# Two gaps between on-chip buffers: a split activation tensor begins 64 bytes later

## What is computed

```python
z = u @ w_in                                       # 2048 x 11264
merged = gate_a * (y_a @ w_branch_a) + gate_b * (y_b @ w_branch_b)
h = h + merged @ w_out                             # 2048 x 2048
h = h + jnp.square(jax.nn.relu(u @ w_up)) @ w_down # 2048 x 8192 x 2048
proj = jnp.einsum('bld,dc->blc', hn, w_in[layer])  # 2048 x 6656
y = jnp.einsum('blc,cd->bld', jnp.concatenate([ya, yb], axis=-1), w_out[layer])
```

## Time and profile before

| | |
|---|---|
| Median of 3 runs | 1893.94 us |
| Lowest, highest | 1893.53, 1894.71 us |
| Profiled execution, first to last instruction | 1893.3 us |
| TensorE matmuls busy | 1879.6 us (99%) |
| VectorE, ScalarE, GpSimd busy | 1101.4, 889.3, 143.6 us |
| Mean granted TensorE clock | 0.999 |
| DMA | 346.47 MB, 183 GB/s |

### The profile page before, as it was taken

The page is one execution under the profiler, slowest core; times in us unless marked ns, Lnnn a source line. Parts: engine busy times, 40 slices in busy tenths (PEclk is TensorE's granted clock), DMA queues, the critical chain, the costliest instruction groups (busy, mean ns, idle before and its releaser), DMA issues.

```text
span 1893.3 us, 33876 instructions
## 1 busy us (share of the span) xinstructions
PE 1879.6 (99%) x13432; PEld 1743.7 (92%) x13432; DVE 1101.4 (58%) x1270; ACT 889.3 (47%) x1171; POOL 143.6 (8%) x122
## 2 busy tenths in 40 slices
PE   9999999999999999999999999999999999999998
PEld 9989998999999889988998899899889999899986
DVE  6556766667655555545445445445565556767664
ACT  6544444455544445443444344334454355664543
POOL 2001322411001100000010000000010000000000
PEclk9999999999999999999999999999999999999999
DMA  8566565566565656656665665566556655354454
GB/s 270 184 181 177 181 179 178 165 200 180 168 231 191 214 186 179 194 198 192 196 192 193 194 191 194 194 190 190 189 185 181 179 170 150 105 147 144 156 190 143
DMA packets 176434, 346.47 MB, mean 183 GB/s; under 512 B 10976, under 2 KB 11184, under 8 KB 175776
## 3 DMA queue, kind: packets, MB, share of 16 engines
q1 hardware_dynamic: 174176, 337.76, 57.2%
q0 software_dynamic: 2128, 6.82, 1.4%
HBM read 342.44 MB, written 2.10 MB: 182 GB/s over the span
## 4 chain that ended last, share of the span: by engine, by line
PE 97%; DVE 1%; ACT 0%; DMA 0%; issue 0%; SPq 0%; DVEq 0%; ACTq 0%
PE ps L446 58%; PE ps L458 33%; PE ps L548 1%; PE ps L781 1%; DVE wlo L1301 1%; PE ps L771 1%; PE ps L748 1%; PE ps L791 0%; DMA raw<-in_w_in_dram 0%; ACT whi L899 0%; PE ps L476 0%; PE ps L759 0%; PE ps L599 0%; PE ps L591 0%; DVE xlo L1323 0%; PE ps L610 0%
## 5 line engine op out<-in xcount | busy, mean ns | idle before, releaser
L1301 DVE TENSOR_TENSOR wlo<-raw,whi 128x1024 fp32r<-128x1024 f32 x631 | 796.5, 1268 | 698.1 <-ACT whi L899 697.1
L899 ACT ACTIVATE whi<-raw 128x1024 fp32r<-128x1024 f32 x631 | 664.5, 1058 | 886.3 <-PE ps L446 551.5
L446 PE MATMUL ps<-xhi,whi 128*128 128x256 f32 (+1 forms) x1904 | 542.2, 285 | 0.4 <-DVE wlo L1301 0.3
L446 PE MATMUL ps<-xhi,wlo 128*128 128x256 f32 (+1 forms) x1904 | 531.3, 279 | 0.0
L446 PE MATMUL ps<-xlo,whi 128*128 128x256 f32 x1664 | 462.5, 278 | 0.0
L446 PEld LDWEIGHTS ps<-xhi,whi 128*128 128x128 f32 x1904 | 359.1, 189 | 9.3 <-issue 6.7
L446 PEld LDWEIGHTS ps<-xhi,wlo 128*128 128x128 f32 x1904 | 357.8, 188 | 0.0
L446 PEld LDWEIGHTS ps<-xlo,whi 128*128 128x128 f32 x1664 | 313.4, 188 | 1.5 <-issue 0.7
L446 PE MATMUL ps<-x2hi,whi 128*128 128x256 f32 x1024 | 282.8, 276 | 0.0
L446 PE MATMUL ps<-x2hi,wlo 128*128 128x256 f32 x1024 | 282.7, 276 | 0.0
L446 PE MATMUL ps<-x2lo,whi 128*128 128x256 f32 x1024 | 282.7, 276 | 0.0
(11 more groups left out here) (373 smaller groups left out, 2370.6 us busy)
## 6 DMA issues: line engine op xcount, KB each, us to landing
raw<-in_w_in_dram SPq DMA_DIRECT2D x279, 512.0 KB, 3.8
raw<-in_w_up_dram SPq DMA_DIRECT2D x128, 512.0 KB, 3.7
raw<-in_w_down_dram SPq DMA_DIRECT2D x128, 512.0 KB, 3.7
raw<-in_w_out_dram SPq DMA_DIRECT2D x64, 512.0 KB, 3.8
raw<-in_w_branch_a_dram SPq DMA_DIRECT2D x16, 512.0 KB, 4.9
raw<-in_w_branch_b_dram SPq DMA_DIRECT2D x16, 512.0 KB, 3.8
x_nat<-in_x_dram SPq DMA_DIRECT2D x4, 512.0 KB, 7.4
rel<-in_rel_turned_dram POOLq DMA_DIRECT2D x8, 256.0 KB, 4.3
```

What stands on the lines that cost most here:

```text
L446: ins = mm(outs[b], w[:, k % SLOTS, j, cols], v, start=start, stop=last and j == CK - 1 and i == 2, skip_group_check=True)
L899: f(whi[:, k % SLOTS], raw[:, k % SLOTS], ACT.Copy).then_inc(whi_ready, 1)
L1301: tt(wlo[:, k % SLOTS], raw[:, k % SLOTS], whi[:, k % SLOTS], ALU.subtract).then_inc(wlo_ready, 1)
```

## The change

`x_place` grows from 48 to 64 elements per partition (192 to 256 bytes) and `arena_place` (64 bytes) goes. `xhi` and `xlo` so begin 64 bytes later. Everything behind them stays where it was, and no instruction, wait or load changes but for the addresses of x.

```diff
@@ -35,8 +35,7 @@
 CK = 2
 NC = KT // CK
 SLOTS = 4
-X_PLACE = 48
-ARENA_PLACE = 16
+X_PLACE = 64
 LEAD = 4
 TW = 320
 WIDE_FIRST = 12
@@ -127,7 +126,6 @@
         sb("x_place", [P, X_PLACE])
         xhi = sb("xhi", [P, KT, TM], F32R)
         xlo = sb("xlo", [P, KT, TM], F32R)
-        sb("arena_place", [P, ARENA_PLACE])
         x_flat = [v[:].rearrange("p k t -> p (k t)") for v in (xhi, xlo)]
         uhi, ulo = [v[:, 0:KT * T].rearrange("p (k t) -> p k t", k=KT) for v in x_flat]
         mhi, mlo = [v[:, KT * T:KT * TM].rearrange("p (k m) -> p k m", k=KT) for v in x_flat]
```

## The result

The change makes the kernel slower: 1923.53 us (1922.66 to 1923.82, five runs) against 1893.53 (1892.09 to 1894.71, five runs), a ratio of 1.0155, 95% interval 1.0143 to 1.0167. That is 30.0 us, where I had forecast 7.1. The profiled execution took 1923.53 us and spans 1921.3, 28.0 more than the span before.

What follows compares the result with a forecast made beforehand. The prediction took TensorE's matmul spacing to bound the kernel. From a median of 1893.9 us it added 7.1 us for long fast spells of x, all else 0, giving 1901.0 us; range 1887 to 1911.

Steps and rivals of the forecast that it cites:

- What bounds the kernel: TensorE's matmuls, busy 1879.6 of 1893.3 us; only their spacing or holes between them could move the time by much.
- Places: Modulo 256 bytes, rings begin at 0, x and the arena at 192; the change takes x to the rings' 0.
- Instructions, writers, cost 0: No instruction, wait or queue changes; ScalarE's and VectorE's writes of x cost 0, within 0.6 us either way.
- Streams of x: TensorE's 256-column matmuls reading x: 1,608 in long fast spells go from 113.4 to 117.8 ns, 7.1 us more.
- slow stretches: Runs of x matmuls already at 117.8 ns, 1,488 in all, were to stay slow; 6.5 us off if they sped up.
- short chunks: Pieces of x matmuls between attention steps, said to be set anew each time and left out of the sum.
- wide stage: 144 matmuls of 272 columns at 123.3 ns, 10.0 above their columns' 113.3; used only to size x's possible loss, 11.6 us.
- natural chunks: 768 matmuls of 512 columns streaming a ring over x were to stay; bound 3.4 us more.
- The bounds: For streamed x: 6.5 us off if the slow spacing went, 15.4 us more if all 3,504 fast matmuls became slow.
- x2 "stays": Sign of being right: x2's streamed matmuls in the feed-forward keep 87.07 us for 768.
- The reason I gave: Slower likelier: streams beginning at one place have the least distance, and 3,504 fast matmuls can rise, 1,488 slow ones fall.
- Its rival: Place doesn't matter to TensorE's matmuls: 1893.9 us, between 1892.5 and 1895.5; chance 0.30.

Runs made afterwards that it cites:

- the second version: The first version with three spare transposes added at the start of feed-forward quarters 2 to 4; 1897.80 us, ratio 1.0020 to the kernel before.
- the first version: The kernel before with the feed-forward's hidden layer and `yt`, which only natural chunks read, moved to offset 0 modulo 256; 1900.41 us, ratio 1.0030.

## Why the prediction was wrong in size

**What bounds the kernel** was read rightly: with TensorE busy nearly throughout, 28.3 us more of its busy time became 28.0 us of span.

**Places.** The sizes were right, with the arena at 192. The experiment that moved the rings shows what they decide: the relation of the streamed buffer to the ring sets the pace.

**Instructions, writers, cost 0:** right. `xhi`'s first blocks are written as before (median 482 ns), by this line on the tile `xhi` in the kernel after:

```profile
L925 ACT ACTIVATE xhi<-ps,mix_w x16: 458/482/539, 7.4 to 19.5; 128x256 fp32r<-128x256 f32 x16
```

**Streams of x, the step that failed.** I wrote: "I take the value between: the long fast spells of x [...] go to the slow one." I let the change choose only between the two spacings that the trace held, 113.4 and 117.8. It brought a third, 120.0, and for all x matmuls. So the term of 1,608 x 4.4 = 7.1 us was too small in its price and in its count. The same matmuls paid 6.6 ns, 10.6 us. The slow stretches, which I left slow, paid 2.2 more, 2.5 us. The short chunks, which I left out as "set anew each time", paid as well: 2.1 us before the branches, and 5.5 in the second block, whose score matmuls with 64 rows stayed at 0.66 us a group. The branches' 168 added 1.1. With the terms below (the wide stage's 2.8, natural chunks' -1.6, x2's 5.1) and the 0.2 us earlier start, this adds up to 27.9 of the 28.0 us of span.

**The bounds.** My bound for the streams took the matmuls at 113.4 ns to 117.8 (15.4) and stopped there; 6.6 ns for 3,504 and 2.2 for 1,488 would have been 26.4. I had a row for a larger excess, the wide stage's 10.0 ns, and used it for a smaller number than the known spacing gave, when it could have told me that spacings beyond the two exist.

**The wide stage** had no term. It grew by 3.1 ns a matmul, 2.6 us in the piece of 840 and 2.8 in all.

**Natural chunks:** I bounded them by 0 and 3.4 us more. They gained 2.1 ns each, 768 x 2.1 = 1.6 us less.

**x2 "stays":** true of three quarters, wrong of the first, where a slow spell was caught on entry for 5.1 us. I had the rows for it in the spells of the earlier trace rows, but I asked only of the stages that read x which spell they would be in.

**The reason I gave** for more time rather than less was two streams with the least distance at one place. It is half right at best: 0 is the slowest of the six for streamed x, but 64, 128, 160 and 224 are slow too, and at one place the natural form is at its quickest. What the six places show is that 192 was the odd one out, not that 0 was. The direction was right with this reason, and so partly by luck.

**The rule weighed against it** was the second, independent read port for the weight load in the Trainium skill's "SBUF — State Buffer", under the bandwidth-pool intuition. That no place could matter with it was my inference; this case's runs disagree with it, since moving the rings by 192 bytes against untouched streams took 113.4 to 120.0 ns. Its rival had 0.30. By the Trainium skill's "TensorE: Matmul & The Clock Gate", on the back-to-back gap of an isolated matmul, an estimate for 256 columns is 109.2 ns. No place reached it with a weight load for each matmul, 113.3 being the best seen.

Of what I named beforehand as signs, "wrong in size if a spacing other than 113.4 and 117.8 comes up" came true. In part so did a sign of being wrong in kind, "in stages that don't read x": x2's first quarter has 5.1 of the 28.0 us.

## What to carry to other kernels

In this kernel the buffer that matmuls stream and the buffer that their weights come from had a best offset modulo 256 bytes among the six tried. It differed between the streamed form (192) and the natural one (0), and 32 bytes beside it cost 4 to 7 ns a matmul. Where your matmuls likewise run at nearly one column per cycle and each loads its own weights, measure the offsets in steps of 32, each form by itself. Read the pace from pieces of the chain divided by their counts, since busy times hide it, and when an edit touches timing, look at the stages it doesn't touch: a spell caught on entry cost 5 us here, and can turn the gain of one form into a loss in the next. When pricing an unknown relation, don't take the states seen before as the only ones.

## What was unexpected of the hardware

- Moving one buffer by 64 bytes costs 1.55%, with no engine waiting for a new thing: 113.4 to 120.0 ns a matmul of 256 columns.
- Offsets of 0 and 256 bytes give the same paces, and a step of 32 bytes is visible: 160, 192 and 224 give 117.3, 113.4 and 118.3 ns in the pieces of 192.
- Counted in columns of 2.4 GHz, three matmuls in a row exceed their columns by 48, 80 or 96 (113.3, 117.8 and 120.0 ns), and natural ones by 96, 112 or 144 (226.7, 228.9 and 233.3 ns). All are multiples of 16 columns, 64 bytes of the streamed buffer. The streamed paces of 128, 160 and 224 are not (86, 77 and 84), and what lies behind it no run shows.
- At place 0 all long pieces of x run at one pace, 120.0; at 192 there are two, 113.4 and 117.8, and a stage keeps the one that it enters with, as long as no other instruction comes between. The chain of the second version has the same first matmuls as the first version's, at another pace (the first version took 31.09 for them):

```profile
30.16 29.94 PE ps L452 x264
```

- The runs fit this: 20 of the kernel before on one chip spread from 1892.18 to 1896.00 us, and four with x at 64, always in one spell before x2, from 1913.92 to 1914.24. That the spread comes from spells chosen anew in each execution isn't shown, since one execution of each kernel has a trace.
- One moved buffer, a third of the reads, costs about half of moving both (ratios 1.0076 and 1.0155).
- The records of the weight loads show what a spell is. These are the loads before x's matmuls in the slow spell of the kernel before (35 to 60 us; least, median, greatest ns):

```profile
L446 PEld LDWEIGHTS ps<-xhi,whi x72: 187/188/188, 34.9 to 60.0; 128*128 128x128 f32 x72
L446 PEld LDWEIGHTS ps<-xlo,whi x71: 192/192/192, 35.0 to 59.7; 128*128 128x128 f32 x71
L446 PEld LDWEIGHTS ps<-xhi,wlo x71: 187/188/188, 35.1 to 59.9; 128*128 128x128 f32 x71
```

One load in three is always the long one. In the fast spell (70 to 100 us) none is, all three kinds have 187 to 188 ns. In the slow quarter of x2 in the kernel after (770 to 830 us) it is again one of three, there the one before `x2hi` x `whi`. At place 0 (70 to 100 us of the kernel after) all are long:

```profile
L444 PEld LDWEIGHTS ps<-xhi,whi x84: 192/192/192, 69.9 to 99.7; 128*128 128x128 f32 x84
```

What stays open: why a load takes 188 or 192 ns at a given offset, what decides on entry whether one of three is long, and why neighbours of a moved read pay a part. No run here tells these apart.
